# Sparse heads' value products on the two column halves of the array

## What is computed

```python
def _dsa_attention(q, k, v, iq, iw, ik, q_pos, k_pos, bias_table):
    ...                                        # index scores, top_idx
    s = jnp.einsum('bqhd,bqkd->bqhk', q, k_sel) * HEAD_DIM ** -0.5
    ...                                        # + bias, mask
    p = jax.nn.softmax(s, axis=-1)
    o = jnp.einsum('bqhk,bqkd->bqhd', p, v_sel)    # 8 heads, one shared v of 64 columns
    return o.reshape(B, Tq, DSA_WIDTH)
```

## Time and profile before

| | |
|---|---|
| median of 3 runs | 2510.47 us (2506.95 to 2513.23) |
| profiled execution, own time | 2504.2 us |
| its span, first to last instruction | 2502.4 us |
| TensorE busy | 2435.7 us, 97% |
| VectorE busy | 1441.7 us, 58% |
| ScalarE busy | 1044.7 us, 42% |
| mean granted TensorE clock | 0.995 |

### The profile page before, as it was taken

The page is one execution under the profiler, slowest core; times in us unless marked ns, Lnnn a source line. Parts: engine busy times, 40 slices in busy tenths (PEclk is TensorE's granted clock), DMA queues, the critical chain, the costliest instruction groups (busy, mean ns, idle before and its releaser), DMA issues.

```text
span 2502.4 us, 36218 instructions
## 1 busy us (share of the span) xinstructions
PE 2435.7 (97%) x13547; PEld 2104.8 (84%) x13547; DVE 1441.7 (58%) x2875; ACT 1044.7 (42%) x1811; POOL 268.3 (11%) x364
## 2 busy tenths in 40 slices
PE   7999999999999999998899999999999999999998
PEld 7999999978877678777788988999979889888887
DVE  5544444464257458887544468888875635444444
ACT  4322222233234346656433457876555533222221
POOL 1100000014210001110013200000100001000000
PEclk9999999999999999999899999999999999999999
DMA  6212121233357353333424542322321132322331
GB/s 234 81 68 85 68 85 68 85 134 110 122 163 247 113 158 123 100 115 88 175 68 148 166 146 72 101 87 73 94 61 51 37 144 84 133 93 86 102 101 67
DMA packets 169323, 271.28 MB, mean 108 GB/s; under 512 B 72032, under 2 KB 104832, under 8 KB 169152
## 3 DMA queue, kind: packets, MB, share of 16 engines
q0 software_dynamic: 43200, 167.29, 19.8%
q1 hardware_dynamic: 125952, 101.68, 12.8%
HBM read 235.21 MB, written 35.29 MB: 108 GB/s over the span
## 4 chain that ended last, share of the span: by engine, by line
PE 88%; DVE 4%; issue 3%; DMA 2%; ACT 1%; SPq 1%; DVEq 0%; POOL 0%; ACTq 0%
PE bank L1403 14%; PE bank L1405 14%; PE bank L1404 14%; PE bank L1420 7%; PE bank L1421 7%; PE bank L1422 7%; PE bank L1440 5%; PE bank L1442 5%; PE bank L1441 5%; PE bank L1532 3%; PE bank L1501 2%; PE bank L1502 1%; PE bank L1515 1%; PE bank L1460 1%; DMA rows<-o_scr 1%
## 5 line engine op out<-in xcount | busy, mean ns | idle before, releaser
L1993 DVE TENSOR_TENSOR w_lo<-raw,w_hi 128x1024 fp32r<-128x1024 f32 x320 | 385.9, 1216 | 135.4 <-ACT w_hi L1707 134.9
L1403 PE MATMUL bank<-XTh_a,w_hi 128*128 128x320 f32 x1408 | 440.4, 313 | 2.8 <-DVE w_lo L1993 2.5
L1405 PE MATMUL bank<-XTh_a,w_lo 128*128 128x320 f32 x1408 | 436.1, 310 | 0.0
L1404 PE MATMUL bank<-XTl_a,w_hi 128*128 128x320 f32 x1408 | 436.0, 310 | 0.0
L1707 ACT ACTIVATE w_hi<-raw 128x1024 fp32r<-128x1024 f32 x320 | 332.0, 1047 | 217.3 <-PE bank L1442 127.5
L1420 PE MATMUL bank<-w_hi,hid_hi 128*128 128x512 f32 x792 | 317.9, 401 | 10.9 <-DVE X_a L2024 5.4
L1421 PE MATMUL bank<-w_lo,hid_hi 128*128 128x512 f32 x792 | 312.6, 395 | 0.0
L1422 PE MATMUL bank<-w_hi,hid_lo 128*128 128x512 f32 x792 | 310.4, 392 | 0.0
L1403 PE MATMUL bank<-XTh_b,w_hi 128*128 128x512 f32 x704 | 282.8, 402 | 0.0
L2024 DVE SCALAR_TENSOR_TENSOR X_a<-bank,X_a 128x512 f32<-128x512 f32 x220 | 151.1, 689 | 224.2 <-PE bank L1422 223.5
L1404 PE MATMUL bank<-XTl_b,w_hi 128*128 128x512 f32 x704 | 278.3, 395 | 0.0
(11 more groups left out here) (326 smaller groups left out, 3954.6 us busy)
## 6 DMA issues: line engine op xcount, KB each, us to landing
raw<-in_w_gate POOLq DMA_DIRECT2D x44, 1024.0 KB, 5.6
raw<-in_w_up POOLq DMA_DIRECT2D x44, 1024.0 KB, 5.7
raw<-in_w_down POOLq DMA_DIRECT2D x44, 1024.0 KB, 5.2
raw<-in_w_in POOLq DMA_DIRECT2D x16, 1024.0 KB, 5.4
s_k_in<-in_cache_diff_k SPq DMA_DIRECT2D x16, 512.0 KB, 4.5
s_v_in<-in_cache_diff_v SPq DMA_DIRECT2D x8, 1024.0 KB, 5.9
raw<-in_w_out POOLq DMA_DIRECT2D x8, 1024.0 KB, 5.5
q_rows_b<-q_scr SPq DMA_DIRECT2D x80, 64.0 KB, 2.0
```

What stands on the lines that cost most here:

```text
L1403: pe.matmul(out, hi[:, k], XTh[g][:, k, lo:up], start=(k == 0), stop=False)
L1404: pe.matmul(out, hi[:, k], XTl[g][:, k, lo:up], start=False, stop=False)
L1405: last = pe.matmul(out, low[:, k], XTh[g][:, k, lo:up], start=False, stop=(k == KD - 1))
L1993: dve.tensor_tensor(hilo(w_lo, u)[:, :, 0:width_of(u)], raw_part(u), hilo(w_hi, u)[:, :, 0:width_of(u)].bitcast(F32), ALU.subtract).then_i ...
```

## The change

For a `dsa` block the two calls of `weigh` become one. The values of a tile of keys are the weights (64 columns) and the transposed probabilities (128 columns) move; head 0's result goes to partitions 0 to 63 of the bank, that is the left column half of the array, head 1's to partitions 64 to 127, the right half, and the two heads alternate tile by tile. The result stands transposed (value column by query). So ScalarE copies it from the bank to a free slot of the value buffer (`o_flip`), TensorE transposes it (`o_turn`, one pass) and VectorE takes it from there (`o_take`, unchanged work). `o_turn` and `o_take` of a block stand in the next iteration, after the next block's scores. The probabilities of a block now have four buffers in all (`pT` and `pT_more`, which lies over free slots of the key buffer), so that the copy for one block waits for the product two blocks before it. `PACE` has new numbers, and the planner's durations for these items are new, so main pieces stand in other places in both attention stretches.

The diff, cut to its core:

```diff
-PACE = ({'x': 0, 'dx': 0.5, 'idx': 1.6, 'diff': 1.2, 'dsa': 1.7, 'end': 0.7},
-        {'idx': 1.2, 'diff': 1.0, 'dsa': 1.5, 'end': 1.5})
+PACE = ({'x': 1.6, 'dx': 1.1, 'idx': 1.6, 'diff': 1.3, 'dsa': 1.3, 'end': 0.9}, {'idx': 0.9, 'diff': 1.7, 'dsa': 1.5, 'end': 1.0})
...
+                a["pT_more"] = lay_a("pT_more", [P, K_RING, LEN // P, P])
...
+        def turned_o(b):
+            return A[BLOCKS[b][3]]["v"][:, 1 - values_no(b) % 2, b % 2]
...
                 def weigh(b, n):
...
+                    else:
+                        for e, (lo, up) in enumerate(fours(t)):
+                            for head in range(2):
+                                emptied(pe, ("probs", b, head, e))
+                            for k in range(lo, up):
+                                for head in range(2):
+                                    last = pe.matmul(out_of(key)[head * HD:(head + 1) * HD, 0:P], a["v"][:, m % 2, k, 0:HD],
+                                                     probs_T(b, head)[:, k], start=(k == 0), stop=(k == t))
+                    last.then_inc(fills(key), 1)
+
+                def o_turn(b):
+                    key = ("ot", b)
+                    emptied(pe, ("o", b))
+                    vacant(pe, key)
+                    pe.transpose(out_of(key)[:, 0:P], turned_o(b), ident[:]).then_inc(fills(key), 1)
...
+                def o_flip(b):
+                    key = ("o", b)
+                    done(act, key)
+                    if b - 2 > LAST_DIFF[BLOCKS[b][3]]:
+                        done(act, ("ot", b - 2))
+                    act.activation(turned_o(b), out_of(key)[:, 0:P], ACT.Copy).then_inc(frees(key), 1)
...
                 def o_take(b):
-                    key = ("o", b)
+                    key = ("o" if kind == "diff" else "ot", b)
```

More of the change, by code:

```diff
@@ L183 @@
             PASS_NO[_b, _a] = len(PASS_NO)
-        for _a in range(1 if _blk[0] == "diff" else 2):
-            SET_NO[_b, _a] = len(SET_NO)
-SETS = list(SET_NO)
+LAST_DIFF = tuple(max(b for b, blk in enumerate(BLOCKS) if blk[0] == "diff" and blk[3] == g) for g in (GA, GB))
 DIFF_NO = {b: n for n, b in enumerate(b for b, blk in enumerate(BLOCKS) if blk[0] == "diff")}
@@ L331, in needs @@
         if kind == "weigh":
-            return [("probs",) + item[1:]]
+            return [("probs", item[1], a) for a in range(2)]
+        if kind == "o_flip":
+            return [("weigh", item[1], 1)]
+        if kind == "o_turn":
+            return [("o_flip", item[1])]
         if kind == "o_take":
-            return [("weigh", item[1], a) for a in range(2)]
+            return [("o_turn", item[1]), ("weigh", item[1], 0)]
         if kind == "o_square":
@@ L373, in steps @@
         kind = item[0]
-        if kind in ("q_turn", "q_low", "score", "raise", "mix", "probs", "weigh", "o_take", "o_square", "o_store"):
+        if kind in ("q_turn", "q_low", "score", "raise", "mix", "probs", "weigh", "o_flip", "o_turn", "o_take", "o_square", "o_store"):
             form, n, t, g = BLOCKS[item[1]]
@@ L392, in steps @@
             if kind == "weigh":
-                return [("PE", (0.28 if form == "diff" else 0.15) * (t + 1))], 1 - item[2]
-            return [{"o_take": ("DVE", 0.45), "o_square": ("ACT", 0.5), "o_store": ("DVE", 0.4)}[kind]], 0
+                return [("PE", 0.25 * (t + 1))], 1
+            if kind == "o_turn":
+                return [("PE", 0.2), ("DVE", 0.0)], 1
+            return [{"o_flip": ("ACT", 0.45), "o_take": ("DVE", 0.45), "o_square": ("ACT", 0.5), "o_store": ("DVE", 0.4)}[kind]], 0
         if kind in ("search", "settle", "mark", "count"):
@@ L420 @@
                "reload": 1.0, "fence": 3.0, "x_o_store": 3.0, "x_norm": 4.0}
-    HOLDS = {"q_low": "q_turn", "low": "turn", "o_take": "weigh"}
+    HOLDS = {"q_low": "q_turn", "low": "turn", "o_take": "weigh", "o_flip": "weigh"}
     def ready(self, item):
@@ L461, in side @@
             self.free += [t] * banks
-        if item[0] in self.HOLDS:
+        if item[0] in self.HOLDS and (item[0] != "o_take" or BLOCKS[item[1]][0] == "diff"):
             self.free[self.held.pop((self.HOLDS[item[0]],) + item[1:])] = t
@@ L623, in att_items @@
             scores(b, 0)
+        if att2 and BLOCKS[b - 2][0] == "dsa":
+            out.append(("o_turn", b - 2))
         counting()
@@ L638, in att_items @@
         counting()
+        if att2 and BLOCKS[b - 2][0] == "dsa":
+            out.append(("o_take", b - 2))
         if i < n:
@@ L653, in att_items @@
         if att1:
-            out.append(("o_take", b - 1))
+            out.append(("o_take" if BLOCKS[b - 1][0] == "diff" else "o_flip", b - 1))
         if i < n and BLOCKS[b][0] != "idx":
@@ L1330, in build, with probs_T @@
         x_time = {"n1a": 16, "n1b": 16}
+        def probs_T(b, n):
+            kind, _, t, g = BLOCKS[b]
+            if kind == "diff":
+                return A[g]["pT"][:, b % 2]
+            if (b - LAST_DIFF[g]) % 2:
+                return A[g]["pT"][:, n]
+            spare = [x for x in range(K_RING) if x != keys_no(b, n) % K_RING]
+            return A[g]["pT_more"][:, spare[n]]
+        def turned_o(b):
+            return A[BLOCKS[b][3]]["v"][:, 1 - values_no(b) % 2, b % 2]
         o_slot = {b: n for n, b in enumerate(b for b, blk in enumerate(BLOCKS) if blk[0] != "idx")}
```

52 lines of the change are left out of this document (21 added, 31 removed).

## The result

The changed kernel takes 2525.6 us (median; 2523.9 to 2533.0) where the kernel before takes 2509.9 beside it: 1.0072, 95% interval 1.0061 to 1.0084. It is slower by 0.7%; the forecast was 2494.

What follows compares the result with a forecast made beforehand. TensorE, busy 97% of the span, was taken as the bound. Terms -19.1 + 1.6 - 3 + 16 - 11 - 6 + 5 = -16.5 took the median 2510.47 to 2494 us; forecast case 2481 to 2503, 8-in-10 range 2478 to 2510.

Steps and rivals of the forecast that it cites:

- Product: Sparse heads' product on TensorE: 288 pairs at 0.109 us, 31.4 us, replace 576 passes taking 64.2 us.
- changes of division: TensorE around each sparse product: switching the array's division and back, 32 blocks x 2 x 0.16 = 10.2 us.
- -19.1 + 1.6 - 3: Whole product change: net TensorE saving -19.1 us, last blocks of each group +1.6, VectorE's moved waits -3.
- Halves don't take turns: Rejects the rival for the 288 pairs that halves take turns: 0.218 us a pair, +31.4, 2525 us; chance 0.06.
- loads of 64 columns don't stand between passes: Rejects the rival that weight loads stand between the product's passes: 0.056 us each, +16, 2510 us; chance 0.03.
- What is added elsewhere: Outside TensorE: `o_flip` on ScalarE costs +1.6 us at group ends; the product wait leaving VectorE gives -3 (0 to -10).
- If TensorE waits for `o_flip` inside the blocks: Sign of being wrong, in the sparse blocks: `o_flip` was to be on the path only in each group's last block.
- Seven samples: Stretch 749.6 to 819.9: 16 main pieces leave, about 58 us long, loss +10 us (0 to +22).
- other samples: Remaining samples' stretch: 12 main pieces leave, loss +3 us (0 to +8).
- before the first score: Stretch before the first sample score: 14 main pieces leave, loss +3 us (0 to +8).
- sparse blocks: Group A's sparse blocks: 24 more main pieces fill idle time, -11 us (0 to -16), under 4 us idle left.
- behind `leave`: After group A's `leave`: 8 more main pieces give 11 us of cover, -6 us (0 to -10).

Runs made afterwards that it cites:

- early `o_take`: Changed kernel with a sparse block's `o_take` directly behind `o_turn` instead of behind `q_low` on VectorE: 2506.4 us, 0.9990 of the kernel before.
- the old product in the new places: Kernel before with every main piece between the same side items as in the changed kernel: 2527.7 us, 1.0072.
- new places in A only: Kernel before with the changed kernel's main-piece places in group A's stretch and the old ones in group B's: 2507.6 us, 0.9994.
- late `o_take`: The changed kernel's own order, `o_take` behind `q_low` on VectorE: 2525.6 us; with the main pieces placed as in the kernel before, 2551.5 us.
- turning the order over: New product, `o_turn` and `o_take` behind the first head's transposes, queries' turn behind the second's: 2518.0 us with group B's places old, 2527.2 with both groups' old.
- mixed places: Changed kernel with `o_take` directly behind `o_turn` and group B's main pieces where the kernel before had them, group A's places new: 2500.4 us, 0.9972.

## Why the prediction was wrong

- **Product, right.** 0.109 us a pair and 1.9 us for the long block, as worked out from the strips and the half. All 576 passes from first pass to next instruction take 39.9 us with 3.2 of waits for `o_flip` in them (behind the last two blocks of each group), 36.7; the forecast was 31.4 and half of the 10.2 for changes of division, 36.5. In the new places the product with early `o_take` gains 2527.7 - 2506.4 = 21.3 us; the sum had -19.1 + 1.6 - 3 = -20.5. That so much shows is partly luck: the mean clock is 0.989 in the one run and 0.991 in the other, at most some 5 us, and with group B's old places far less shows.
- **The rivals on the array, refuted.** Halves don't take turns (the time that rival gave, 2525, is the measured one, by accident), and loads of 64 columns don't stand between passes. The Trainium skill ("TensorE: Matmul & The Clock Gate", Part 3, The mechanism) lets a load overlap with running matmuls only for another row group, though the same section also has loads into a background weight buffer go ahead; here both halves have the same rows, and 32 passes with 32 loads take 1.89 us. The trace doesn't agree with the first; it agrees with the other rule of the Trainium skill ("TensorEngine Tiling (Array Packing)", Key Properties), that different tiles can load and multiply in parallel.
- **"What is added elsewhere", wrong: the largest miss.** I took -3 us (0 to -10, +3 if ScalarE gets late) and said that `o_take` does the same work. It does, and it no longer waits for the product on VectorE: that wait, 26.6 us in the earlier trace rows, is gone from this place. But `o_take` also empties a bank, and I followed only who is queued behind the waiting instruction on its engine, not who waits for the bank: +19.2 us (early `o_take`, shown), so the term is set wrong by about 22. "If TensorE waits for `o_flip` inside the blocks" stood among the signs of being wrong; it does, 5.6 us, but the larger wait was for the step behind.
- **Places in group A, right in its terms, wrong on idle time.** Seven samples: forecast 58 us, measured 58.9, +10.8 beyond main work where I had +10; other samples +3.0 (forecast +3), before the first score +2.5 (+3), sparse blocks with the old product 66.4 to 56.9, -9.5 (-11), behind `leave` -6.7 (-6). Alone they cost nothing: 2507.6. VectorE was 46.2 of 58.9 us busy, 78% (forecast over 75). The clock behind the sparse blocks is 1.00, as forecast. TensorE idles 21.2 us in the sparse blocks of the changed kernel, and 7 with the old product in the new places, where I had under 4. The sparse blocks of the changed kernel took 118.6 us where I had some 90; my 90 counted from 1135.5 and this stretch from the turn of the first sparse queries (1123.4 before), which is 12 us, and another 12 are the wait for `o_take` (71.4 against 59.2 in the table).
- **Places in group B, wrong.** I costed only the end behind `leave`, +5 (measured +4.8, and "some us idle" there is 4.3 of 22.0), and left the differential blocks (166 to 149 pieces) and the sparse blocks (33 to 44) at nothing. All together cost 20 us with the old product; in its profiled execution 12 lie in the differential blocks and 6 to 7 in the sparse ones. No term held that the clock falls there, either. The table of pieces showed the move; VectorE at 285.3 of 336.6 us in the differential blocks before would have shown that it had little room.

Sum of the steps by medians: places in A -0.6 (2507.6 against 2508.2), in B +20.1, product -21.3, late `o_take` +19.2: +17.4, where the change measures +15.7. These are differences along one row of runs, so that they add up proves nothing (the 1.7 is the kernel before, 2508.2 and 2509.9 in two places). The terms depend on each other: with group B's old places the product gains 7 to 11 us and not 21.

VectorE in group B's differential blocks of the kernel before, and of the changed one above:

```profile
1489.00:1825.60 336.60, 330.47 (x2057) 307.34 (x2056) 285.33 (x681) 240.59 (x395) 28.59 (x46) 1.00 0.28 88
```

What stays open is why the product gains 10 us less in group B's old places. The passes themselves gain as much there: from first pass to next instruction group B's take 46.0 us with the old product and 27.4 with the new one (new places in A only, early `o_take`), and with new places in both groups 47.4 and 28.1. The difference is what TensorE waits for around them. Group B's sparse blocks with the new product, new places in A only and then in both:

```profile
1833.70:2001.30 167.60, 150.28 (x1160) 124.14 (x1158) 113.16 (x302) 102.36 (x201) 5.91 (x10) 1.00 0.17 49
...
1824.70:2009.10 184.40, 172.72 (x1322) 150.82 (x1320) 123.14 (x319) 115.08 (x217) 7.81 (x12) 0.99 0.19 56
```

Against the lines with the old product, TensorE's idle time rises with the old places from 11.2 to 17.3 us; with the new ones it falls from 13.5 to 11.7, and the clock rises from 0.96 to 0.99. With the old places the waits name ScalarE's copies, `o_flip` and `q_low` in turn, and turning the order over put others in their place.

## What to carry to other kernels

When a product gets another layout and with it more steps behind it, follow the buffer of each new step to whoever takes it next, through every engine's queue: a step that costs nothing on its own engine can hold the bank that the bound engine needs. Set the step that empties a shared bank ahead of everything on its engine that waits for a third engine. And price every stretch whose number of filler pieces changes, above all one where a second engine is 85% busy, not only those where the numbers look large. Before a difference between two runs is put down to waits, compare TensorE's idle time and its granted clock in the same stretch.

## What the runs showed of the hardware

- fp32 passes on two column halves with the same rows run at once, loads included: 0.109 us a pair, as one pass alone. Eight passes of one half and then eight of the other still overlap in part (2.49 us for 32 passes; 3.5 would be none).
- The granted clock in the seven samples was 0.94 where it had been 1.00, with TensorE busy 51.9 of 58.9 us and before 70.3 of 70.3, and behind `leave` of group B 0.90 and before 1.00: both are means over the two levels, 2.4 and 1.2 GHz, so a part of each stretch ran at the lower one. Main pieces taken out of a stretch can show in the clock too, but not in every execution: the run with the mixed places and early `o_take` has the same few pieces in the seven samples, TensorE busy 48.9 of 56.7 us, and a clock of 1.00 there.
- The same idle time can go with very different clocks: in group A's sparse blocks TensorE idled 20 us in two runs, at 0.78 and at 0.94, and the first took 13.4 us longer.
